# Weight sums of a Strassen feed-forward by adding transfers from DRAM, and a scheme that begins two blocks earlier

## What is computed

```python
D_FF = 4 * D_MODEL                     # 4096

def sqrelu_mlp(h, w1, w2):
    return jnp.square(jax.nn.relu(h @ w1)) @ w2
...
        x = x + sqrelu_mlp(rms_norm_2(x, norm_ffn[i]), ffn_w1[i], ffn_w2[i]).astype(x.dtype)
```

## Time and profile before

| | us |
|---|---|
| three timed runs | 2618.2, 2624.03, 2622.53 (median 2622.53) |
| profiled execution | 2618.97 |
| its span | 2617.2 |
| TensorE busy | 2580.0 |
| VectorE busy | 1687.4 |
| ScalarE busy | 1286.9 |
| GpSimd busy | 505.9 |

### The profile page before, as it was taken

One profiled execution on the slowest core, in us unless ns is written; L12 is line 12 of the kernel. 1 busy time (PEld: TensorE's weight loads), 2 busy tenths in 40 slices (PEclk: granted clock), 3 DMA queues, 4 the chain that ended last, 5 costly groups with the idle time before them and its releaser, 6 DMA issues. The chain is left out here.

```text
span 2617.2 us, 35132 instructions
## 1 busy us (share of the span) xinstructions
PE 2580.0 (99%) x12530; PEld 2044.8 (78%) x12530; DVE 1687.4 (64%) x2288; ACT 1286.9 (49%) x2138; POOL 505.9 (19%) x366
## 2 busy tenths in 40 slices
PE   9999999999999999999999999999999999999999
PEld 7855788888786557788888776789988787889887
DVE  4476677643988785677653787588743536688633
ACT  3326543333547894444333587457533424557432
POOL 0020100000104781100000130035810002045800
PEclk9999999999999999999999999999999999999999
DMA  5320222222234442222222220133232321223222
GB/s 212 105 80 17 100 96 97 97 98 96 81 131 129 121 129 80 82 96 96 96 97 96 95 73 1 58 105 113 81 110 97 102 88 52 94 108 114 81 96 96
DMA packets 72991, 248.39 MB, mean 95 GB/s; under 512 B 8076, under 2 KB 8204, under 8 KB 72496
## 3 DMA queue, kind: packets, MB, share of 16 engines
q1 hardware_dynamic: 71792, 238.53, 27.2%
q0 software_dynamic: 944, 8.40, 0.9%
q10 hardware_dynamic: 144, 0.00, 0.0%
HBM read 242.56 MB, written 2.24 MB: 94 GB/s over the span
## 5 line engine op out<-in xcount | busy, mean ns | idle before, releaser
L356 DVE TENSOR_TENSOR wlo<-wraw,whi 128x1024 fp32r<-128x1024 f32 x353 | 454.9, 1290 | 421.1 <-ACT whi L333 420.0
L382 PE MATMUL bank<-hnhi,whi 128*128 128x512 f32 (+1 forms) x1664 | 654.0, 393 | 2.0 <-DVE arena L1972 1.2
L383 PE MATMUL bank<-hnlo,whi 128*128 128x512 f32 (+1 forms) x1664 | 638.3, 384 | 0.0
L333 ACT ACTIVATE whi<-wraw 128x1024 fp32r<-128x1024 f32 x361 | 380.1, 1055 | 485.3 <-DMA wraw<-in_w 485.1
L384 PE MATMUL bank<-hnhi,wlo 128*128 128x512 f32 x1536 | 598.5, 390 | 0.0
L382 PE MATMUL bank<-ahi,whi 128*128 128x512 f32 x1184 | 463.1, 391 | 0.9 <-DVE alo L605 0.4
L384 PE MATMUL bank<-ahi,wlo 128*128 128x512 f32 x1184 | 460.8, 389 | 0.0
L383 PE MATMUL bank<-alo,whi 128*128 128x512 f32 x1184 | 460.7, 389 | 0.0
L382 PEld LDWEIGHTS bank<-hnhi,whi 128*128 128x128 f32 x1664 | 312.7, 188 | 93.7 <-issue 32.8
L383 PEld LDWEIGHTS bank<-hnlo,whi 128*128 128x128 f32 x1664 | 312.9, 188 | 63.8 <-issue 4.8
L384 PEld LDWEIGHTS bank<-hnhi,wlo 128*128 128x128 f32 x1536 | 288.3, 188 | 61.8
(11 more groups left out here) (351 smaller groups left out, 3908.8 us busy)
## 6 DMA issues: line engine op xcount, KB each, us to landing
wraw<-in_w SPq DMA_DIRECT2D x410, 512.0 KB, 3.3
arena<-cs_scratch SPq DMA_DIRECT2D x20, 512.0 KB, 5.7
over_a<-cs_scratch SPq DMA_DIRECT2D x12, 512.0 KB, 5.9
arena<-in_rpb POOLq DMA_DIRECT2D x1, 2880.0 KB, 14.1
out_dram<-xT SPq DMA_DIRECT2D x8, 256.0 KB, 2.0
arena<-in_t_step POOLq DMA_DIRECT2D x2, 897.0 KB, 5.7
mT<-arena SPq DMA_DIRECT2D x28, 64.0 KB, 2.0
arena<-in_t_ab POOLq DMA_DIRECT2D x1, 1472.0 KB, 6.7
```

The lines of the kernel that those rows point to most:

```text
L333: act.activation(whi[:, slot * BLOCK:(slot + 1) * BLOCK], wraw[:, slot * BLOCK:(slot + 1) * BLOCK], ACT.Copy).then_inc(sem("w_hi"), 1)
L356: dve.tensor_tensor(low_home(i), wraw[:, slot * BLOCK:(slot + 1) * BLOCK], whi[:, slot * BLOCK:(slot + 1) * BLOCK], ALU.subtract).then_inc ...
L382: pe.matmul(out, wh, ah, start=start, stop=False)
L383: pe.matmul(out, wh, al, start=False, stop=False)
```

## The change

The sums s1 to s4 of the weight quarters are no longer made by GpSimd's arithmetic. GpSimd issues transfers instead, five for each pair, of 256 KB each: a21 is loaded from DRAM into a quarter of `over_a` (one of four, by n % 4), and a22, a11 and a12 are fetched from DRAM and added to it on the way, which makes s1, then s2, then s4 in the same place, each after the low part of the one before has been made. s3 is made in the block's own slot by adding a11 to the a21 that lies there. As only additions are used, signs change: s2 = s1 + a11, s3 = a11 + a21, s4 = a12 + s2, with t1 to t4, copy_z, sum_w and sum_c changed to match. A semaphore for each of the four places counts the landings. s2 and s3 of a pair may land in either order, so the high part of either waits for a count of 64, which stands for both.

PLAIN goes from 8 to 6, so there are 13 pairs instead of 12. The parts of s3 and s4 take the place of block 2's and that of a22 block 3's. The steps that make t1 to t4 and the first pair's parts are put at other points of the six plain blocks, and the lows of t3 and t4 go into the first pair. SyncE loads a block when the quarters of its own slot are split, without a wait for a sum. The product steps of TensorE and their order in a cycle are the same. Some semaphores are merged and renamed (`moved`, `v_banked`, `v_turned`), and the order in which "mlp_down" takes its banks follows the odd number of pairs.

```diff
-PLAIN = 8
+PLAIN = 6
...
-        SPLIT = pair_counts([s for c in range(PAIRS) for s in (before(("a11", 0), ("s1", 0), ("a12", 0)) if c == 0 else [])
-                             + [("s2", c)] + (before(("a22", 0)) if c == 0 else [])
-                             + before(("a11", c + 1), ("s1", c + 1), ("s3", c), ("s4", c), ("a12", c + 1), ("a22", c + 1))])
+        SPLIT = pair_counts([(q, 0) for q in ("a11", "s1", "a22", "a12")]
+                            + [s for c in range(PAIRS) for s in [("s2", c)] + before(
+                                ("a11", c + 1), ("s1", c + 1), ("s3", c), ("s4", c), ("a12", c + 1), ("a22", c + 1))])
...
+        SUM_STEPS = {"a21": 16, "s1": 32, "s2": 64, "s3": 64, "s4": 80}
...
-        def sum_raw(q):
-            return over_a[:, SUM_AT[q] * SEQ:(SUM_AT[q] + 1) * SEQ]
+        def sum_raw(f, q, n):
+
+            if q == "s3":
+                return block_raw(f, n, "a21")
+            return over_a[:, n % 4 * QUARTER:(n % 4 + 1) * QUARTER]
+
+        def wait_sum(eng, f, q, n):
+            before = len(range(n % 4, PAIRS, 4)) * f + n // 4
+            eng.wait_ge(sem(f"block_sum{n % 4}"), 80 * before + SUM_STEPS[q])
...
-            freed, half = {"a11": (4, 0), "s1": (4, 1), "a12": (5, 0), "s2": (5, 1), "s3": (6, 0), "s4": (6, 1),
-                           "a22": (7, n % 2)}[q]
+            freed, half = {"a11": (4, 0), "s1": (4, 1), "a12": (5, 0), "s2": (5, 1), "s3": (2, 0), "s4": (2, 1),
+                           "a22": (3, n % 2)}[q]
...
-                sp.wait_ge(sem("w_lo"), split(f, "a22", n))
-                sp.wait_ge(sem("sum_pool"), pool_summed(f, "s4", n))
+                sp.wait_ge(sem("w_lo"), max(split(f, q, n) for q in (("a22", "s3") if (i - first_pair(f)) % 2 else ("a11", "a12"))))
...
+            def fetched(q, n):
+                i = first_pair(f) + 2 * n + (q in ("a21", "a22"))
+                a = (q in ("a12", "a22")) * QUARTER
+                return A["w"][i:i + 1, :, a:a + QUARTER]
+
+            def load_sum(n):
+                if n >= 4:
+                    pool.wait_ge(sem("w_lo"), split(f, "s4", n - 4))
+                if n < PAIRS:
+                    pool.dma_start(sum_raw(f, "s1", n), fetched("a21", n)).then_inc(sem(f"block_sum{n % 4}"), 16)
+
+            def add_sum(q, n):
+
+                if n >= PAIRS:
+                    return
+                if q in ("s1", "s3"):
+                    wait_sum(pool, f, {"s1": "a21", "s3": "s1"}[q], n)
+                if q == "s3":
+                    wait_block(pool, f, n, 1)
+                if q in ("s2", "s4"):
+                    pool.wait_ge(sem("w_lo"), split(f, {"s2": "s1", "s4": "s2"}[q], n))
+                pool.dma_start(sum_raw(f, q, n), fetched({"s1": "a22", "s2": "a11", "s3": "a11", "s4": "a12"}[q], n),
+                               accum_op=ALU.add).then_inc(sem(f"block_sum{n % 4}"), 16)
+
             pool.wait_ge(sem("sum_pool"), POOL_SUMS * f + 1)
-            pool.wait_ge(sem("sum_dve"), DVE_SUMS * f + 1)
+            pool.wait_ge(sem("sum_dve"), summed(f, "t3"))
+            for n in range(3):
+                load_sum(n)
+            for q, n in (("s1", 0), ("s1", 1), ("s3", 0), ("s2", 0)):
+                add_sum(q, n)
             for n in range(PAIRS):
...
+                add_sum("s4", n)
+                add_sum("s2", n + 1)
+                add_sum("s1", n + 2)
+                add_sum("s3", n + 1)
+                load_sum(n + 3)
...
-                act.activation(pair_bank(n, "z"), pair_bank(n, "x"), ACT.Copy).then_inc(sem("sum_copied"), 1)
+                act.activation(pair_bank(n, "z"), pair_bank(n, "x"), ACT.Copy, scale=-1.0).then_inc(sem("sum_copied"), 1)
...
-                elif m <= 5:
+                elif m <= 3:
                     act_next(act, name, At(m))
                 if m == 1:
+                    token_high("t1")
+                if m == 2:
+                    token_high("t2")
                     token_high("t3")
-                if m == 2:
-                    token_high("t1")
+                if m == 4:
+                    high("a11", 0)
+                    high("s1", 0)
+                    high("a22", 0)
+                if m == 5:
+                    high("a12", 0)
                 hidden_square(m)
-                if m == 4:
-                    token_high("t2")
+                if m == 3:
                     token_high("t4")
...
+                if m == 0:
+                    tokens("t2")
+                    tokens("t3")
                 if m == 2:
-                    tokens("t2")
                     tokens("t4")
                 if m == 3:
-                    token_lows("t3")
                     token_lows("t1")
-                if m == 5:
                     token_lows("t2")
-                    token_lows("t4")
-                if m == 6:
+                if m == 4:
                     low("a11", 0)
                     low("s1", 0)
+                    low("a22", 0)
...
                 if n:
                     sum_c(n - 1)
+                else:
+                    token_lows("t3")
                 low("s3", n)
                 if n == 0:
                     sum_w(0)
                 low("s4", n)
+                if n == 0:
+                    token_lows("t4")
...
-                    pe.wait_ge(sem("mlp_relu"), relu_done(f, (4, 7)[n] if n < 2 else PLAIN + 2 * (n - 2)))
+                    pe.wait_ge(sem("mlp_relu"), relu_done(f, (4, 3)[n] if n < 2 else PLAIN + 2 * (n - 2)))
```

More of the change, by code:

```diff
@@ L979, in pool_pairs @@
-            for n in range(PAIRS):
[L980 to L988, removed]
-                pool.tensor_tensor(sum_raw("s2"), sum_raw("s1"), block_raw(f, n, "a11"), ALU.subtract)\
-                    .then_inc(sem("sum_pool"), 1)
-                if n:
-                    pool.wait_ge(sem("w_lo"), split(f, "s3", n - 1))
-                pool.tensor_tensor(sum_raw("s3"), block_raw(f, n, "a11"), block_raw(f, n, "a21"), ALU.subtract)\
-                    .then_inc(sem("sum_pool"), 1)
-                if n:
-                    pool.wait_ge(sem("w_lo"), split(f, "s4", n - 1))
-                pool.wait_ge(sem("sum_pool"), pool_summed(f, "s2", n))
-                pool.tensor_tensor(sum_raw("s4"), block_raw(f, n, "a12"), sum_raw("s2"), ALU.subtract)\
-                    .then_inc(sem("sum_pool"), 1)
@@ L1133, in tokens @@
             def tokens(t):
-                half = slice(0, HALF_N) if t == "t4" else slice(HALF_N, SEQ)
                 if t == "t3":
-                    dve.wait_ge(sem("sum_copied"), COPIES * f + 1)
+                    dve.wait_ge(sem("sum_dve"), summed(f, "t2"))
+                    b = over_a[:, :].rearrange("p (k s) -> p k s", k=4)
+                    t3, t2 = (mT[:, token(s)].rearrange("p (k s) -> p k s", k=4) for s in ("t3", "t2"))
+                    dve.tensor_tensor(t3, b[:, :, 0:HALF_N], t2, ALU.subtract).then_inc(sem("sum_dve"), 1)
+                    return
                 if t == "t2":
                     dve.wait_ge(sem("sum_pool"), POOL_SUMS * f + 1)
-                if t == "t4":
-                    dve.wait_ge(sem("sum_dve"), DVE_SUMS * f + 2)
+                else:
                     dve.wait_ge(sem("norm_sum"), norm + 1)
+                half, other, op = (slice(HALF_N, SEQ), "t1", ALU.add) if t == "t2" else (slice(0, HALF_N), "t2", ALU.subtract)
                 for j in range(4):
-                    less = over_a[:, j * SEQ + HALF_N:(j + 1) * SEQ] if t == "t3" else mT[:, token("t1" if t == "t2" else "t2", j)]
                     ins = dve.scalar_tensor_tensor(out=mT[:, token(t, j)], in0=xt(4 + j)[:, half], scalar=col(g, g0 + 4 + j),
-                                                   in1=less, op0=ALU.mult, op1=ALU.subtract)
+                                                   in1=mT[:, token(other, j)], op0=ALU.mult, op1=op)
                 ins.then_inc(sem("sum_dve"), 1)
@@ L1198, in dve_mlp_up @@
                 low("s2", n)
-                if n == 0:
-                    low("a22", 0)
                 if n + 1 < PAIRS:
@@ L1209, in dve_mlp_up @@
                 low("s4", n)
+                if n == 0:
+                    token_lows("t4")
                 if n + 1 < PAIRS:
                     low("a12", n + 1)
+                    low("a22", n + 1)
                 else:
                     dve_split(dve, At(FIRST[f"mlp_down{f}"]))
-                if n + 1 < PAIRS:
-                    low("a22", n + 1)
             sum_w(PAIRS - 1)
```

98 lines of the change are left out of this document (41 added, 57 removed).

## The result

The changed kernel is slower. Its four timed runs have a median of 2774.78 us (2774.08 to 2779.87), the kernel before 2621.54 in the same number of runs: a ratio of 1.0592, with an interval of 1.058 to 1.0605, or 153 us. The forecast was 2616 with 2609 to 2632.

A forecast was written before the change was run, and what follows sets the result against it. TensorE, busy 99% of the span, was taken as the bound. Pairs −1.6, holes −3.8 + 1.0, clock −1.5 and a later hole −0.6 gave −6.5 us, from 2622.53 to 2616.0, range 2609 to 2632 (8 in 10).

The forecast's parts named there:

- Part 1: MLP stages: one more pair replaces two plain blocks on TensorE, gaining 0.81 us a stage, 1.6 in all.
- The two token lows (t3, t4): VectorE, first pair: 1.2 us each, costed at nothing as made while ScalarE waits; uncovered, up to 1.2 on the hole.
- Part 2: Sums leave GpSimd: five transfers a pair replace four additions, 3.6 us of issuing hidden; the price is latency, taken as 4.
- L: Latency of a GpSimd adding transfer from issue to landing: taken as 4 us, between 2.9 and about 5.5.
- Rival 1: Pairs' start: latency near 5.4 us keeps a 1.9 us hole in both stages, clock as now; 2620.9 us, chance 0.24.
- Part 3: Pairs' start: whether the new chain holds TensorE up; a 0.5 us hole in each stage, later cycles 4.3 us more room.
- the path that I called tighter: Pairs' start: s2(1) and s3(1) through ScalarE to sum_c(0); latency 3.5 us just holds, 4 makes a 0.5 hole.
- Rival 2: DMA engines become the bound; at adding cost 3 times plain a pair takes 12.7 us, total 2684; chance 0.15.
- x: Cost of an adding transfer relative to a plain one: expected 2, engines become the bound from 2.1.
- Rival 3: GpSimd's issues wait for VectorE; at 2.9 us each a pair takes 14.5, +115 us, 2731; chance 0.05.
- hidden beside everything: GpSimd's five transfer issues, 0.7 us each, 3.6 of a pair's 10.08 us, were claimed to cost nothing.
- The sum: Whole kernel: −1.6 (pairs) − 3.8 + 1.0 (holes) − 1.5 (clock) − 0.6 = −6.5 us; own range 2611 to 2619.5.

The follow-up runs named there:

- e_poolsums: Changed kernel with s1 to s4 made by GpSimd's additions as in the kernel before, SyncE's loads waiting for s4 again: 2622.84 us, ratio 1.0010.
- h_early: e_poolsums with one VectorE step moved, sum_c(0) ahead of the low part of s1(2): 2618.46 us, ratio 0.9994 to the kernel before.
- b_plain: Changed kernel with the four adding transfers of a pair made plain, overwriting, so the sums are wrong: 2688.10 us, ratio 1.0258 to the kernel before.
- a_drain: Changed kernel with GpSimd waiting for its own first multiplication by the norm's factor before queuing the second: 2721.12 us, ratio 1.0384 to the kernel before.
- bd_plain_drain: Changed kernel with both adding transfers made plain and GpSimd waiting for its first multiplication: 2619.29 us, ratio 0.9997 to the kernel before.
- c_own: a_drain with s3 counting on its own semaphore, so the high part of s2 waits for s2 alone: 2642.86 us, ratio 1.0084 to the kernel before.
- i_before_early: Kernel before with one VectorE step moved, sum_c(0) ahead of the low part of s1(2): 2616.53 us, ratio 0.9986.
- f_ahead: Kernel before with an unneeded 64 KB transfer issued by GpSimd ahead of its 32 multiplications in each stage: 2687.74 us, ratio 1.0256.

## Why the prediction was wrong, step by step

- **Part 1, the extra pair** (−1.6). e_poolsums has it and is no faster than before, h_early neither (0.9994, interval up to 1.0004). The sum may be right, but it isn't free of the start: two plain blocks less are 10.9 us less in which sums, token parts and first lows can be made, and the holes at the start grew from 1.7 to 3.1 us a stage. That the shorter cover is the reason is argued, not tried. The two token lows (t3, t4) that I costed at nothing are part of that schedule; how much of the 3.1 is theirs wasn't tried.
- **Part 2, L = 4 us, bounds 2.9 to 5.5.** This is the step that failed first. The medians are 7.4 us (all adding transfers, L997) and 9.0 (s3 alone), the span 3.6 to 11.1. The low end fits a plain transfer at the front of its burst: in b_plain's window 1780 to 1850 s4 lands in 2.9 to 3.0 us. L = 4 fits the adding one in the same place, 4.0 to 4.5 in after. Rival 1 of the prediction had the reason in hand, three issued in a row and the third done 4.5 us after the first begins, and even this counted neither the a21 load behind them nor the 512 KB block loads beside them. In b_plain L997's four, plain, land in 3.7 us (median; s3 alone 5.2), with the engines 0.68 busy. So the latency isn't a constant that can be read from single transfers: it depended on what each one moves and on its place in the burst.
- **Part 3, "in later cycles this way has 4.3 us more room".** Together with part 2 this cost the most, 87 (b_plain) to 102 us (a_drain to bd_plain_drain). I checked one cycle against TensorE's demand, as if the chain began anew each time. But the issue waits for the low part of s1, which waits on ScalarE behind s2, which waits for the issue before: a loop of 1.08 + L + 3.26 us. It must fit in 10.08, so L may be at most 5.7, where my check left 3.5 + 4.3 = 7.8; with 9.4 it turns in 13.8. The range of L that I gave, 2.9 to 5.5, would have fitted just, so the loop alone would not have moved the forecast; with a bound from a burst it would have been the main rival. At the start the same step holds, by the path that I called tighter: its hole is L less 3.5. In bd_plain_drain s3(1) has L = 6.2, which gives 2.7, and 2.3 were measured; in after it has 10.9, which gives 7.4, and TensorE waited 6.4 for copy_z(1). There only L was wrong.
- **Rival 2, x.** Decided from 2.1, measured about 2.2: this was sized well. The Trainium skill, Collectives: The Full Stack, in "The bandwidth ceiling", has adding at half the rate of plain; the 1.62 against 0.75 us here is near that and a little dearer. But the mechanism wasn't the one at work: with a share of 0.73 the engines weren't the bound in the kernel after. They would be next: c_own has 0.91, and at x = 2.2 the rival's own sum gives 10.3 us a pair against 10.08.
- **Rival 3, issues held up by VectorE.** Didn't occur. The issues of L997 took 862 to 1612 ns (s3's the longest) and started 0.54 us apart in a burst, where I had taken 0.7. The estimate from the Trainium skill, SBUF — State Buffer, in "SBUF: two separate sides", 3.5 us an issue, is not borne out here: its figure was taken beside a copy, and VectorE's lows are subtractions of two inputs.
- **What I didn't see at all** (54 to 69 us): the multiplications behind the last issue. I listed five issues a pair at nothing, "hidden beside everything", and never asked what the instruction behind the last of them does. The order on GpSimd at the stage's end changed from addition, multiplication to issue, multiplication. No row of the prediction has that order, and its price wasn't bounded.
- **The sum.** For the holes and the clock it had −3.8, −1.5 and −0.6, 5.9 us in all. i_before_early removes the holes and gains 3.6, so the holes were sized about right, and of the slow clock's 1.5 nothing shows between the medians. It was wrong that transfers were the way. A slip beside it: the low end of the sum's own range, 2611, is taken from 2612.5; from 2616, like the high end, it would be 2615.

Of the signs that I named, TensorE's waits in each pair and longer landing times were given for rival 2 together with a DMA share near 1. They came without that share, which is what separates a loop's latency from an engine's limit.

## What to carry to other kernels

When a change puts a transfer between an engine's step and its next turn, write down the loop, not the first cycle: the sum around it, with the latency of the whole burst issued together, must be below the period. Where several results land on one count, whoever needs only the first pays for the last. And look at what runs behind a newly issued transfer on the same engine, for that costs nothing until it does; a hole at one place is often had for the move of one operation, which should be tried before the work is rebuilt.

## What the runs showed of the hardware

- **A run of GpSimd operations queued right behind the issue of a transfer shut VectorE out for its whole length.** One 128x512 operation of VectorE on on-chip memory took 31.47 us in after and 34.76 in f_ahead (0.69 otherwise), with GpSimd's operations 1.22 to 1.23 us apart; both times it ended 0.55 us behind the last one whose input was ready. With a wait for the first of them in between, they stand 1.63 to 1.67 apart and VectorE gets its turns (1.31 us). The Trainium skill, SBUF — State Buffer, in "SBUF: two separate sides", calls the port pair of the two an exclusive lock, in which one waits while the other's operation runs; the rows agree and go beyond it, for here VectorE didn't get its turn between one operation and the next, 28 and 30 times in a row. Why an issue ahead brings this about and a wait ends it, the runs don't show; that GpSimd has the next operation ready without a free moment is an inference from 1.22 against 1.67.
- **An adding transfer of 256 KB from DRAM takes 1.62 us of the 16 engines' time, a plain one 0.75**. In after, from 1780 to 1850, it lands in 4.0 to 4.5 us as the first of its burst (s4; 2.9 to 3.0 in b_plain, where it is plain) and in 9.4 to 10.5 as s3, behind three others. The last s4 of the first stage, with no other transfer of GpSimd's under way but two block loads issued from 1908 to 1913, took 5.8, so the place in the burst isn't all.
- **The clock falls with such standstills.** It was granted at 0.56 in the 20 us around the end of the long one and at 0.95 from 1780 to 1850, where TensorE was busy 56.37 of 70 us; c_own, with TensorE 67.34 of 70 busy, kept 1.00.
